# Feed-forward layers: the last two accumulating weight units go through the PSUM banks together instead of one after the other

## The reference

```
...
def _squared_relu_mlp(h, w1, w2):
    return jnp.square(jax.nn.relu(h @ w1)) @ w2
...
        x = x + _squared_relu_mlp(_rmsnorm(x, norm_ffn_g[i]), ffn_w1[i], ffn_w2[i])
...
```

## Time and profile before

| | us |
|---|---|
| median of 3 runs | 1189.81 (1189.61 to 1192.93) |
| profiled execution | 1189.99 |
| its span, first to last instruction | 1188.2 |
| PE busy | 1105.8 (93%) |
| DVE busy | 714.2 (60%) |
| ACT busy | 560.8 (47%) |
| PE's share of the chain that ended last | 81% |

### The profile page before, as it was taken

The page is one execution under the profiler, slowest core; times in us unless marked ns, Lnnn a source line. Parts: engine busy times, 40 slices in busy tenths (PEclk is TensorE's granted clock), DMA queues, the critical chain, the costliest instruction groups (busy, mean ns, idle before and its releaser), DMA issues.

```text
span 1188.2 us, 20772 instructions
## 1 busy us (share of the span) xinstructions
PE 1105.8 (93%) x8770; PEld 1073.3 (90%) x8770; DVE 714.2 (60%) x973; ACT 560.8 (47%) x697; POOL 28.5 (2%) x24
## 2 busy tenths in 40 slices
PE   5896688999999999999999998997789999999997
PEld 4886678999999889999999998997689999999997
DVE  2664534645446777777556666568976647644554
ACT  3446324544434655535435445698444316344441
POOL 0102210000000000000000000000000000000000
PEclk9898789999999999999999998998999999999999
DMA  9243212555575365646555563323200044655521
GB/s 297 77 137 106 71 36 72 185 186 190 183 282 177 113 212 171 212 143 191 201 177 182 176 205 110 124 72 107 71 2 1 1 131 153 215 182 189 190 74 35
DMA packets 116959, 167.51 MB, mean 141 GB/s; under 512 B 5792, under 2 KB 97568, under 8 KB 116512
## 3 DMA queue, kind: packets, MB, share of 16 engines
q1 hardware_dynamic: 115184, 166.18, 42.8%
q10 hardware_dynamic: 1712, 0.43, 0.2%
HBM read 165.55 MB, written 1.05 MB: 140 GB/s over the span
## 4 chain that ended last, share of the span: by engine, by line
PE 81%; DVE 10%; ACT 5%; issue 3%; DMA 1%; SPq 0%; DVEq 0%; ACTq 0%
PE bank L1850 23%; PE bank L1852 22%; PE bank L1851 22%; DVE sb_w_low L1135 2%; ACT sb_w_high L618 2%; PE bank L2279 1%; DVE sb_arena L1205 1%; PE bank L2356 1%; PE bank L1986 1%; DMA sb_constants<-in_constants 1%; PE bank L1993 1%; DVE sb_arena L1710 1%; DVE sb_state L1707 1%; PE bank L2344 1%; ACT sb_arena L954 1%
## 5 line engine op out<-in xcount | busy, mean ns | idle before, releaser
L1135 DVE TENSOR_TENSOR sb_w_low<-sb_raw,sb_w_high 128x2048 fp32r<-128x2048 f32 x150 | 344.7, 2301 | 276.9 <-ACT sb_w_high L618 276.8
L1850 PE MATMUL bank<-sb_act_high,sb_w_low 128*128 128x256 f32 x1376 | 398.8, 290 | 20.9 <-DVE sb_arena L1194 5.2
L618 ACT ACTIVATE sb_w_high<-sb_raw 128x2048 fp32r<-128x2048 f32 x150 | 285.7, 1911 | 267.5 <-PE bank L1852 267.4
L1852 PE MATMUL bank<-sb_act_high,sb_w_high 128*128 128x256 f32 x1376 | 394.5, 287 | 0.0
L1851 PE MATMUL bank<-sb_act_low,sb_w_high 128*128 128x256 f32 x1376 | 392.6, 285 | 0.0
L1850 PEld LDWEIGHTS bank<-sb_act_high,sb_w_low 128*128 128x128 f32 x1376 | 265.3, 193 | 24.8 <-issue 7.1
L1851 PEld LDWEIGHTS bank<-sb_act_low,sb_w_high 128*128 128x128 f32 x1376 | 267.3, 194 | 0.3 <-issue 0.2
L1852 PEld LDWEIGHTS bank<-sb_act_high,sb_w_high 128*128 128x128 f32 x1376 | 264.5, 192 | 0.0
L1850 PE MATMUL bank<-sb_hidden_high,sb_w_low 128*128 128x256 f32 x896 | 254.3, 284 | 0.7 <-DVE sb_hidden_low L1537 0.7
L1852 PE MATMUL bank<-sb_hidden_high,sb_w_high 128*128 128x256 f32 x896 | 253.4, 283 | 0.0
L1851 PE MATMUL bank<-sb_hidden_low,sb_w_high 128*128 128x256 f32 x896 | 251.3, 280 | 0.0
(11 more groups left out here) (337 smaller groups left out, 1139.7 us busy)
## 6 DMA issues: line engine op xcount, KB each, us to landing
sb_raw<-in_ffn_w SPq DMA_DIRECT2D x64, 1024.0 KB, 5.3
sb_raw<-in_w_up SPq DMA_DIRECT2D x16, 1024.0 KB, 5.4
sb_raw<-in_w_down SPq DMA_DIRECT2D x16, 1024.0 KB, 4.9
sb_raw<-in_sgu_w_in SPq DMA_DIRECT2D x16, 1024.0 KB, 5.3
sb_raw<-in_rwkv_w_rkv SPq DMA_DIRECT2D x12, 1024.0 KB, 5.4
sb_raw<-in_w_in SPq DMA_DIRECT2D x10, 1024.0 KB, 6.8
sb_raw<-in_sgu_w_out SPq DMA_DIRECT2D x8, 1024.0 KB, 4.9
sb_raw<-in_w_out SPq DMA_DIRECT2D x4, 1024.0 KB, 5.4
```

Source lines behind the costliest of these rows:

```text
L618: nc.scalar.activation(whi[s][:], raw[s][:], ACT.Copy).then_inc(hi_done, 1)
L1135: nc.vector.tensor_tensor(wlo[s][:], raw[s][:], f32(whi[s][:]), ALU.subtract).then_inc(lo_done, 1)
L1850: nc.tensor.matmul(dst, l_lo, r_hi, start=start, stop=False, **kw)
L1852: return nc.tensor.matmul(dst, l_hi, r_hi, start=False, stop=stop, **kw)
```

## The change

Units 30 and 31 of each feed-forward are taken together: the function `accumulate_end` waits for both units and both halves, and then goes bank by bank, in each bank first the 12 matmuls of unit 30 and then the 12 of unit 31.

```diff
+        def accumulate_end(u, h):
+
+            parts = [(two(whi[(u + s) % RING][:, :]), two(wlo[(u + s) % RING][:, :])) for s in range(2)]
+            for s in range(2):
+                pe.wait_ge(lo_done, u + s + 1)
+                pe.wait_ge(h_lo, h + s + 1)
+            for b in range(4):
+                for s, (hi, lo) in enumerate(parts):
+                    for n in (2 * b, 2 * b + 1):
+                        cs = slice(n * P, n * P + P)
+                        dst = bank[2 + b][:, (n % 2) * T:(n % 2) * T + T]
+                        for k in range(2):
+                            ins = split_matmul(dst, hi[:, k, cs], lo[:, k, cs], hid_hi[:, 2 * s + k, :],
+                                               hid_lo[:, 2 * s + k, :], start=False, stop=s == 1 and k == 1,
+                                               skip_group_check=True)
+                    if b == 3:
+                        ins.then_inc(w_used, 1)
+                if b < 3:
+                    ins.then_inc(acc_ps, 1)
+
...
             body(0, first=True)
             with pe.Fori(1, FCH - 1) as i:
                 body(i)
-            for s in range(2):
-                pe.wait_ge(h_lo, h0 + 2 * FCH - 2 + s + 1)
-                accumulate(u0 + 4 * FCH - 2 + s, s, last=s == 1)
+            accumulate_end(u0 + 4 * FCH - 2, h0 + 2 * FCH - 2)
```

## The result

| | before | after |
|---|---|---|
| median, us | 1191.89 (1189.61 to 1193.08, 6 runs) | 1196.30 (1193.77 to 1198.14, 6 runs) |
| profiled execution, us | 1189.99 | 1193.77 |
| its span, us | 1188.2 | 1192.0 |

The account below looks back on a forecast made before the run. The prediction took TensorE (PE), busy 1105.8 of 1188.2 us, to bound the kernel. Three feed-forward losses of 1.78, 1.78 and 1.79 us, 5.35 in all, gave 1195.2 us from a median of 1189.81; whole range 1192.8 to 1198.2.

Parts of the forecast that it names:

- The hole: Ahead of unit 30 in each feed-forward, PE would newly wait for half 1, complete 1.61 us after PE's old start.
- The sum: Over the three feed-forwards, losses of 1.78, 1.78 and 1.79 us: 5.35 us in all, giving 1195.2 us, 0.45% slower.
- Both small terms: At unit 30's start: 0.06 us from DVE's end to PE's start, and 0.11 us for the uncovered first weight load.
- Early banks are worth 0: At each feed-forward's end, DVE getting three banks earlier gains 0; in the first, at most 1.36 us.
- The cover of what follows: After the feed-forwards, work starting from PE's end shifts too: second, `high` and logarithm by 1.78 us; third, squares' sums and final norm.
- The clock: Behind the new 1.67 us holes the clock stays, value 0; rival: it falls, 1198.2 us once, 1204.2 thrice, chance 0.06.
- The price of a fall: Behind a hole in PE's work, one clock fall would cost 4 × 0.50 + 4 × 0.25 = 3.0 us.
- Part given back: Rival, chance 0.10: the gating phase gives back 1.36 us (1193.8), or later slack absorbs one whole hole (1193.4).
- No new wait: Rival at unit 30, chance 0.05: half 1 is ready in time and only order changes, 1189.8 us.
- Faster: Rival, chance 0.03: PE's next phase waits for a bank-drain backlog in each feed-forward, so the change saves time, 1182.2 us.
- The range: Whole kernel: forecast's own range 1194.6 to 1195.8 us; whole range 1192.8 to 1198.2 us.
- the measurement's grain: For the whole kernel's time, a measurement can tell from no change about 0.3%, 3.6 us.

Follow-up runs that it names:

- wait alone: Kernel before with its old matmul order, but PE waits for both halves and both units ahead of unit 30; ratio 1.0036 to the kernel before.
- two banks: Changed kernel reordered: banks 2 and 3 with unit 30, then 31, then banks 4 and 5; half 1 awaited after 24 matmuls; ratio 0.9995 to the kernel before.
- second alone: Kernel before with the new order and joint wait in the second feed-forward only; ratio 1.0022 to the kernel before.
- third alone: Kernel before with the new order and joint wait in the third feed-forward only; ratio 1.0009 to the kernel before.
- late wait: Changed kernel, waiting for half 1 and unit 31 only after unit 30's 12 matmuls in bank 2; ratio 0.9997 to the kernel before.
- first alone: Kernel before with the new order and joint wait in the first feed-forward only; ratio 1.0012 to the kernel before.
- early `high`: Kernel before with ACT's rounding of the next part's third weight unit moved ahead of the four squares after the second feed-forward; ratio 0.9985 to the kernel before.
- long hole: Kernel before, but in the first feed-forward PE waits ahead of unit 30 for something 5 us late; ratio 1.0047 to the kernel before.

## Why the prediction was right

- **The hole.** Half 1 was to be complete 1.61 us after unit 30 could have begun. In the changed kernel unit 30 could have begun at 717.02 + 0.12 = 717.14, and L1384 ends at 718.06 + 0.69 = 718.75: 1.61. The wait alone makes the loss, and the wait put at its first use takes away all but 0.40 of the 1.83: shown.
- **The sum.** 1.78 us a feed-forward forecast, 1.82 to 1.83 measured. Both small terms, taken from one row of the gating phase, were a little off. From DVE's end to PE's first matmul the trace has 718.90 − 718.75 = 0.15 us, and not 0.06; the first two matmuls are 0.20 apart, and not 0.23, which is 0.08 more than usual, and not 0.11. PE's loads fit the reading that the second term is the first weight load:

```profile
718.87 0.19 PEld L1850 LDWEIGHTS bank<-sb_hidden_high,sb_w_low 128*128 128x128 f32 x1 [1.78 <-issue]
718.98 0.19 PEld L1851 LDWEIGHTS bank<-sb_hidden_low,sb_w_high 128*128 128x128 f32 x1
```

The load starts 0.03 us ahead of its matmul (718.90), the next one 0.12 ahead of its own (719.10), so 0.09 us of it lies bare. In time, 5.35 us were forecast and 4.8 (2.6 to 6.9) measured. The median of 1196.30 lies 1.1 above the 1195.2 forecast, because the forecast counts from 1189.81, a median of three, and the kernel before had 1191.89 beside the changed one; only the difference bears on the mechanism.
- **Early banks are worth 0.** Shown by the two-bank order. The backlog in the first feed-forward does go (1.3 us; 1.36 was read from the rows), and DVE's end there is 0.47 later where 0.42 was forecast; nobody waits for it, as the restart in the gating phase shows.
- **The cover of what follows.** `high` behind the second feed-forward, the sums of squares and the final norm shifted by the full 1.83 and 1.82: shown.
- **The clock.** Forecast to stay: 1.00 behind all holes of 1.6 us. The price of a fall, 3.0 us, was read a little high: PE idled until 52.51, and 3.49 us at 0.50 and 4 us at 0.75 make 2.7; the one fall that an experiment brought about cost 1.5. The Trainium skill (TensorE: Matmul & The Clock Gate, "HAM oscillation — how this bites in real kernels") tells of a kernel whose waits of some 3 to 5 us ahead of each tile cost it the clock, with every next tile begun at half rate. At 4.91 us the trace agrees, with 0.57. The holes of the change are shorter than the waits told of there, so the Trainium skill does not speak for a fall at 1.60 us.
- **The rivals.** Part given back: no, in the gating phase 0.00 of 1.83. No new wait: no. Faster: no; its condition, a backlog that PE waits for, was in none of the three.
- **The range.** Its own upper end, with the two small terms doubled, should be 1189.81 + 5.35 + 0.51 = 1195.7 and not 1195.8. What I took for the measurement's grain, 0.3%, was coarse: the interval of the ratio is plus or minus 0.18%.

## What to carry to other kernels

When two steps are merged, their waits merge too, and a wait belongs ahead of its first use, not ahead of the group: here 12 matmuls of work ahead of the wait covered 1.44 of its 1.60 us, and 24 covered it all. An earlier hand-over helps only where the receiver is what ends last; see first whether it idles ahead of the last piece. And ask of each buffer release that moves back (here unit 30's, from 48 to 84 matmuls) who could have used it: the trace shows that it was free for today's order of ACT; by the order of the matmuls it would not be for the better one.

## What the runs showed that I had not expected

The third part has two lengths, whatever the kernel. From its first matmul to the `square` of half 1 in the third feed-forward the profiled executions took 431.93 (before), 431.94 (two banks), 431.80 and 431.90 us (second alone, third alone), and 430.74 (after), 430.69, 430.60, 430.70, 430.68 and 430.44 (wait alone, late wait, first alone, early `high`, long hole). The work is the same; the granted clock is not. It falls around the part's first matmul, behind a hole of 3.3 to 3.6 us that PE has there in every kernel. Windows of 1 us at the fall and at the recovery, before and after:

```profile
733.56:734.56 1.00, 0.00 (x1) 0.03 (x1) 0.57 (x2) 1.00 (x3) 0.00 (x0) 0.63 1.11 279
...
740.56:741.56 1.00, 1.00 (x10) 1.00 (x10) 1.00 (x2) 0.53 (x1) 0.00 (x0) 0.96 0.03 4
```

```profile
737.71:738.71 1.00, 1.00 (x7) 1.00 (x8) 1.00 (x4) 1.00 (x4) 0.00 (x0) 0.76 1.11 351
...
740.71:741.71 1.00, 1.00 (x7) 1.00 (x7) 0.84 (x3) 1.00 (x4) 0.00 (x0) 0.53 1.11 350
```

In all windows between these the clock is 0.50. A window at 0.63 holds 0.74 us at 0.50, and so on: before, the clock was low for 0.74 + 6 + 0.08 = 6.8 us, from 0.7 ahead of the first matmul (734.56) to 6.1 behind it; after, for 0.48 + 2 + 0.94 = 3.4 us, from 0.5 to 3.9 behind it (737.71). The same reading gives 6.8 us in all four long executions and 3.4 in all six short ones. Behind the first matmul that is 2.7 us more at half the clock, an estimate of 1.3 us of PE's time; the two lengths differ by 1.2. The stretch ahead of the first feed-forward varies too: its yardstick lies between 379.96 and 383.90 in the ten executions, although the work up to there is the same in all.

The 69 timed runs of the kernel before lie between 1187.5 and 1193.3 us, a spread larger than the whole change. Most of it goes with the mean granted clock of the run. In the group of 31 runs of before, the 8 with 0.974 took 1187.5 to 1188.3 and the 12 with 0.968 took 1191.6 to 1193.3. Compared at 0.974 alone, the medians agree with the yardstick:

| kernel | runs, median | before, same chip | difference | by the yardstick |
|---|---|---|---|---|
| wait alone | 7, 1193.60 | 8, 1187.93 | +5.7 | +5.3 |
| two banks | 7, 1188.20 | 8, 1187.93 | +0.3 | 0.0 |
| third alone | 4, 1189.89 | 14, 1188.32 | +1.6 | +1.8 |
| early `high` | 5, 1188.05 | 3, 1188.19 | −0.1 | −0.3 |

Of the others, the late wait has none at 0.974, and its eight runs at 0.973 have a median of 1189.19, 1.3 above 1187.93, by the yardstick 1.2. The changed kernel (1193.77), first alone and second alone have one such run each, and the long hole none. These are few runs, and they were grouped only after they had been seen.

So an effect of 0.4% is better read from a yardstick inside the trace, or from runs of equal clock, than from two spans or from medians over a mix of clocks. Why an execution has the low clock once for 3.4 us and once for 6.8 stays open: kernels with and without the new holes are in both groups.
